# LayerNorms 1 to 3 carried through the projection that follows them

## What is computed

```python
def layer_norm(x, g, b):
    mu = mean(x); var = mean((x - mu) ** 2)
    return (x - mu) * rsqrt(var + 1e-5) * g + b

def conv_ffn(x, prev, w_up, w_dw, b_dw, w_down):
    g, v = split(x @ w_up, 2)
    g, new_prev = causal_dwconv(g, prev, w_dw, b_dw)
    return (gelu(g) * v) @ w_down, new_prev

# layer 0:  x = layer_norm(a*x + conv_module(x))       LayerNorm 0 inside, LayerNorm 1 here
#           x = layer_norm(a*x + conv_ffn(x))          LayerNorm 2
#           k, v = split(x @ w_kv)
# layer 1:  x = layer_norm(a*x + attention(x @ w_q, k, v) @ w_o)    LayerNorm 3
#           x = layer_norm(a*x + conv_ffn(x))          LayerNorm 4
```

## Time and profile before

| what | value |
|---|---|
| median of 3 runs | 2750.94 us (2749.96 to 2757.99) |
| span of the profiled execution | 2757.9 us (the slowest of the three runs: 2757.99 us) |
| PE busy | 2620.5 us, 95% |
| DVE busy | 1493.9 us, 54% |
| ACT busy | 1166.3 us, 42% |
| POOL busy | 274.9 us, 10% |
| mean granted TensorE clock | 0.969 |

### The profile page before, as it was taken

One profiled execution on the slowest core, in us unless ns is written; L12 is line 12 of the kernel. 1 busy time (PEld: TensorE's weight loads), 2 busy tenths in 40 slices (PEclk: granted clock), 3 DMA queues, 4 the chain that ended last, 5 costly groups with the idle time before them and its releaser, 6 DMA issues.

```text
span 2757.9 us, 48858 instructions
## 1 busy us (share of the span) xinstructions
PE 2620.5 (95%) x17562; PEld 2570.7 (93%) x17562; DVE 1493.9 (54%) x2187; ACT 1166.3 (42%) x1939; POOL 274.9 (10%) x224
## 2 busy tenths in 40 slices
PE   8889697999999999999989989899999999999996
PEld 7888597999999999999978979899999999999996
DVE  6888756544443344454466755654444334444555
ACT  7777635443332333343345433353343223443332
POOL 4888401000000000000010000100000000000001
PEclk9999798999999999999999968999999999999998
DMA  8444243444454344445433312434445434444542
GB/s 271 116 117 127 65 152 99 148 148 152 151 169 146 128 152 149 147 157 177 142 127 112 107 47 97 139 114 148 147 147 174 151 132 144 146 151 151 169 148 78
DMA packets 115061, 382.38 MB, mean 139 GB/s; under 512 B 29472, under 2 KB 29856, under 8 KB 114720
## 3 DMA queue, kind: packets, MB, share of 16 engines
q1 hardware_dynamic: 95328, 373.20, 41.4%
q0 software_dynamic: 992, 6.25, 0.6%
q10 hardware_dynamic: 18688, 2.21, 0.6%
HBM read 375.32 MB, written 8.27 MB: 139 GB/s over the span
## 4 chain that ended last, share of the span: by engine, by line
PE 85%; POOL 8%; DVE 3%; ACT 2%; issue 1%; POOLq 0%; DMA 0%; ACTq 0%; DVEq 0%; SPq 0%
PE acc L377 26%; PE acc L379 26%; PE acc L378 26%; POOL taps_pool L311 8%; PE acc L403 1%; PE acc L404 1%; PE acc L405 1%; DVE xr L1021 1%; ACT xr L728 1%; PE ot L665 0%; PE ot L667 0%; PE pt L564 0%; DVE rows L1034 0%; ACT xh L732 0%; PE pt L496 0%
## 5 line engine op out<-in xcount | busy, mean ns | idle before, releaser
L377 PE MATMUL acc<-xh,w_hi 128*128 128x320 f32 x3968 | 1236.1, 312 | 27.0 <-DVE w_lo L991 25.7
L379 PE MATMUL acc<-xh,w_lo 128*128 128x320 f32 x3968 | 1230.1, 310 | 0.0
L378 PE MATMUL acc<-xl,w_hi 128*128 128x320 f32 x3968 | 1229.7, 310 | 0.0
L685 ACT CAST w_hi<-w_raw 128x1024 fp32r<-128x1024 f32 (+1 forms) x648 | 699.0, 1117 | 556.2 <-PE acc L379 529.0
L991 DVE TENSOR_TENSOR w_lo<-w_raw,w_hi 128x1024 fp32r<-128x1024 f32 (+1 forms) x648 | 828.5, 1318 | 158.6 <-ACT w_hi L685 158.6
L377 PEld LDWEIGHTS acc<-xh,w_hi 128*128 128x128 f32 x3968 | 748.5, 189 | 41.9 <-DVE w_lo L991 32.4
L378 PEld LDWEIGHTS acc<-xl,w_hi 128*128 128x128 f32 x3968 | 748.6, 189 | 0.4
L379 PEld LDWEIGHTS acc<-xh,w_lo 128*128 128x128 f32 x3968 | 748.2, 189 | 0.0
L377 PE MATMUL acc<-hh,w_hi 128*128 128x320 f32 x1408 | 434.9, 309 | 0.0
L378 PE MATMUL acc<-hl,w_hi 128*128 128x320 f32 x1408 | 434.0, 308 | 0.0
L379 PE MATMUL acc<-hh,w_lo 128*128 128x320 f32 x1408 | 434.0, 308 | 0.0
(11 more groups left out here) (186 smaller groups left out, 1563.5 us busy)
## 6 DMA issues: line engine op xcount, KB each, us to landing
w_raw<-in_up SPq DMA_DIRECT2D x352, 512.0 KB, 4.3
w_raw<-in_down SPq DMA_DIRECT2D x128, 704.0 KB, 4.7
w_raw<-in_w_in SPq DMA_DIRECT2D x64, 512.0 KB, 5.9
w_raw<-in_w_out SPq DMA_DIRECT2D x32, 512.0 KB, 4.5
w_raw<-in_w_q SPq DMA_DIRECT2D x32, 512.0 KB, 4.8
w_raw<-in_w_o SPq DMA_DIRECT2D x32, 512.0 KB, 4.1
...
```

The costliest lines, as they stand in the source:

```text
L377: pe.matmul(out, wh, hi[:, k, :], start=first, stop=False)
L378: pe.matmul(out, wh, lo[:, k, :], start=False, stop=False)
L379: mm = pe.matmul(out, wl, hi[:, k, :], start=False, stop=last)
L685: act.copy(w_hi[:, slot, 0:n], w_raw[:, slot, 0:n]).then_inc(hi_ready, 1)
```

## The change

LayerNorms 1, 2 and 3 are no longer finished before the next projection starts. With m the mean and s = 1/std of a token, W(g(x - m)s + b) = s·W(gx) - m·s·Wg + Wb. So:

- While a residual projection runs, ACT and DVE already make the high and low part of z = g·x (with the shift taken off) for each finished tile (`z_hi`, `z_lo`). Two more columns of `xh` and `xl`, numbers 320 and 321, hold g and b (`const_columns`); the matmuls of the up projections, `w_kv` and `w_q` take 322 columns (`TX`) and so give Wg and Wb beside W·z.
- The next projection starts with `project_folded`: two whole groups instead of the batches, tile by tile behind `z_ready`. The two last moment matmuls go inside the first group, behind tiles 1 and 4.
- `norm_rows` makes only the rows `rstd` and `nmr` = -mean·rstd. Every evacuation applies them with the two columns (copied to `cols`): for gates on DVE and ACT through the tiles `gate_x` and `corr`, for values in two fused steps, for k, v and q in `w_kv` and `w_q`.
- The normalised x itself, which the residual needs later, is made by POOL while the next projection runs (`finish_norm`); the next residual addition waits for it (`x_normed`).
- Convolution and attention outputs get input tiles of their own (`conv_hi`, `conv_lo`, `attn_hi`, `attn_lo`), since `xh` and `xl` now hold z during `w_out` and `w_o`; LayerNorm 0 writes there and first waits until the convolution's state is stored. Dummy activations that load ACT's tables write to `table_out`. The scratch for POOL's DMA descriptors is set to 8192.

The core of the diff:

```diff
+TX = T + 2
...
-        xh = sb("xh", [P, KD, T], F32R)
-        xl = sb("xl", [P, KD, T], F32R)
+        xh = sb("xh", [P, KD, TX], F32R)
+        xl = sb("xl", [P, KD, TX], F32R)
...
+            def finish_norm(n):
+                g, b, l = FOLDED[n]
+                pool.wait_ge(rows_ready, n)
+                pool.wait_ge(z_ready, KD * n)
+                for q in range(4):
+                    lo, hi = 4 * q, 4 * q + 4
+                    at = 24 * (n - 1) + 6 * q
+                    pool.tensor_tensor(xr[:, lo:hi, :], xr[:, lo:hi, :], over_tiles(rstd, 4), ALU.mult
+                                       ).then_inc(x_normed, 1)
+                    pool.wait_ge(x_normed, at + 1)
+                    pool.tensor_tensor(xr[:, lo:hi, :], xr[:, lo:hi, :], over_tiles(nmr[:, :], 4), ALU.add
+                                       ).then_inc(x_normed, 1)
+                    pool.wait_ge(x_normed, at + 2)
+                    for k in range(lo, hi):
+                        pool.tensor_scalar(xr[:, k, :], xr[:, k, :], par(g)[:, k + KD * l, :], par(b)[:, k + KD * l, :],
+                                           ALU.mult, ALU.add).then_inc(x_normed, 1)
...
-            center(1, xr)
+            finish_norm(1)
...
-                    pe.matmul(out, wh, hi[:, k, :], start=first, stop=False)
+                    pe.matmul(out, wh, hi[:, k, 0:width], start=first, stop=False)
...
+                    if between and k in between:
+                        between[k]()
...
+            def project_folded(p, n, moments):
+                last_mean, last_square = moments
+                pe.wait_ge(const_cols_ready, n)
+                project_group(p, 0, 0, xh, xl, rhs_wait=(z_ready, KD * (n - 1)), width=TX,
+                              between={1: last_mean, 4: last_square})
+                project_group(p, 0, 1, xh, xl, width=TX)
...
-                        project_first_pair(up, xh, xl, event)
-                        project_pairs(up, xh, xl)
+                project_folded(up, n, moments)
+                project_pairs(up, xh, xl, width=TX)
...
-                pe.wait_ge(bank_read[par_], bank_count(p, pair))
+                pe.wait_ge(q_ready, t + 1)
...
+            def z_hi(n, k):
+                g, _, l = FOLDED[n]
+                act.wait_ge(shifted, KD * n + k + 1)
+                act.activation(xh[:, k, 0:T], xr[:, k, :], ACT.Identity, scale=par(g)[:, k + KD * l, :]
+                               ).then_inc(z_hi_ready, 1)
...
+                        act.wait_ge(cols_ready, 2 * tile + 1)
+                        act.activation(corr[:, :], nmr[:, :], ACT.Identity, bias=cols[:, 0, 1:2], scale=cols[:, 0, 0:1]
+                                       ).then_inc(corr_ready, 1)
+                        split_next(p, i, 0, end, chunks=(1,) if early else (0, 1))
+                        act.wait_ge(gate_ready, tile + 1)
...
+            def z_lo(n, k):
+                g, _, l = FOLDED[n]
+                dve.wait_ge(z_hi_ready, KD * (n - 1) + k + 1)
+                dve.scalar_tensor_tensor(xl[:, k, 0:T], xr[:, k, :], par(g)[:, k + KD * l, :], xh[:, k, 0:T],
+                                         ALU.mult, ALU.subtract).then_inc(z_ready, 1)
...
+            def norm_rows(n, nxt):
+                z_lo(n, KD - 1)
+                dve.wait_ge(moments_ready, n + 1)
+                dve.wait_ge(mean_squared, n + 1)
+                dve.tensor_tensor(rstd, ot[:, 0:T], work[:, 0, :], ALU.subtract).then_inc(var_ready, 1)
+                dve.wait_ge(std_ready, n + 1)
+                dve.reciprocal(rstd, rstd).then_inc(rstd_ready, 1)
+                dve.wait_ge(rstd_ready, n + 1)
+                dve.scalar_tensor_tensor(nmr[:, :], shift, -1.0, rstd, ALU.mult, ALU.mult).then_inc(rows_ready, 1)
+                split_lo(nxt, 0, 1, chunks=(1,))
+                dve.wait_ge(rows_ready, n)
...
-                        dve.tensor_tensor(work[:, 1, :], gy, acc[1][:, 0:T], ALU.mult).then_inc(bank_read[1], 1)
-                        split_next(p, i, 1, end)
+                        dve.tensor_copy(cols[:, 1, :], acc[1][:, T:TX]).then_inc(cols_ready, 1)
+                        dve.tensor_tensor(work[:, 1, :], acc[1][:, 0:T], rstd, ALU.mult).then_inc(bank_read[1], 1)
...
+                        split_next(p, i, 1, end)
```

More of the change, by code:

```diff
@@ L143, in trunk_kernel @@
             pass
-        with nc.sbuf_tensor("k_t", [P, 2, T], F32) as k_t, \
+        with nc.sbuf_tensor("conv_lo", [P, KD, T], F32R) as conv_lo, \
+                nc.sbuf_tensor("conv_hi", [P, KD, T], F32R) as conv_hi:
+            pass
+        with nc.sbuf_tensor("qo", [P, KD, T], F32) as qo, \
+                nc.sbuf_tensor("k_t", [P, 2, T], F32) as k_t, \
                 nc.sbuf_tensor("kc_t", [P, 2, NB, WINDOW], F32) as kc_t, \
@@ L154, in trunk_kernel @@
             pass
+        with nc.sbuf_tensor("attn_lo", [P, KD, T], F32R) as attn_lo, \
+                nc.sbuf_tensor("attn_hi", [P, KD, T], F32R) as attn_hi:
+            pass
         hh = sb("hh", [P, HALF, T], F32R)
         hl = sb("hl", [P, HALF, T], F32R)
+        gate_x = sb("gate_x", [P, T])
+        corr = sb("corr", [P, T])
         acc = [bank("acc0"), bank("acc1")]
@@ L233, in bank_count @@
             return p.base // 2 + ip + 1
[L236 removed]
+        RHS_X, RHS_CONV, RHS_ATTN = (NBT * e for e in range(3))
+        FOLDED = {1: ("mix_g", "mix_b", 0), 2: ("ffn_g", "ffn_b", 0), 3: ("mix_g", "mix_b", 1)}
         def over_tiles(row, n):
@@ L748, in _ @@
             split_hi(ph["w_in"], 1, 0, chunks=(0,))
-            act.activation(rstd[:, 0:1], shift[:, 0:1], ACT.Sigmoid)
+            act.activation(table_out[:, 0:1], shift[:, 0:1], ACT.Sigmoid)
             act.wait_ge(tables_loaded, 32)
@@ L811, in _ @@
             pairs(p, glu_and_square, first=2)
-            act.activation(rstd[:, 0:1], const("eps"), ACT.Sqrt)
+            act.activation(table_out[:, 0:1], const("eps"), ACT.Sqrt)
             act.wait_ge(products_summed, POOL_TAPS)
@@ L818, in _ @@
             conv_square(KD - 1)
-            norm(0, conv_y, ACT.Silu, "norm_g", "norm_b", 0, after[p.name], RHS_CONV)
+            act.wait_ge(state_saved, 16 * KD)
+            norm(0, conv_y, ACT.Silu, "norm_g", "norm_b", 0, after[p.name], RHS_CONV, conv_hi)
             def weights_only(p):
@@ L848, in body @@
                     square(n, 2 * ip + 1, xr[:, 2 * ip + 1, :], work[:, 1, :])
+                    if n in FOLDED:
+                        if end:
+                            last_z_hi(n, p)
+                        else:
+                            z_hi(n, 2 * ip + 1)
                 pairs(p, body, first=1)
             residual(ph["w_out"], 1)
-            norm(1, xr, ACT.Identity, "mix_g", "mix_b", 0, after["w_out"], RHS_MIX0)
+            norm_rows(1, after["w_out"])
             def ffn(l):
@@ L897, in _ @@
             ffn(0)
-            norm(2, xr, ACT.Identity, "ffn_g", "ffn_b", 0, after["down01"], RHS_FFN0)
+            norm_rows(2, after["down01"])
             weights_only(ph["w_kv"])
@@ L976, in _ @@
             for lo, hi in BATCHES:
-                act.copy(xh[:, lo:hi, :], qo[:, lo:hi, :]).then_inc(rhs_hi_ready, 1)
+                act.copy(attn_hi[:, lo:hi, :], qo[:, lo:hi, :]).then_inc(rhs_hi_ready, 1)
             residual(ph["w_o"], 3)
-            norm(3, xr, ACT.Identity, "mix_g", "mix_b", 1, after["w_o"], RHS_MIX1)
+            norm_rows(3, after["w_o"])
             ffn(1)
@@ L1217, in _, with ffn @@
             residual(ph["w_out"], 1.0, 1)
-            norm(1, xr, after["w_out"], RHS_MIX0)
-            def ffn(l, n_norm, rhs):
+            norm_rows(1, after["w_out"])
+            def ffn(l, n_norm):
                 if l:
@@ L1234, in body @@
                         gy_s = work[:, 0, SEQ:T].rearrange("p (n q) -> p n q", q=NQ)
+                        dve.wait_ge(multiplied, group_done(p, i, 0))
+                        dve.tensor_copy(cols[:, 0, :], acc[0][:, T:TX]).then_inc(cols_ready, 1)
+                        dve.tensor_tensor(gate_x[:, :], acc[0][:, 0:T], rstd, ALU.mult).then_inc(bank_read[0], 1)
+                        if not early:
+                            split_next(p, i, 0, end, chunks=(0,))
+                        dve.wait_ge(corr_ready, tile + 1)
+                        dve.wait_ge(bank_read[0], bank_count(p, i))
+                        dve.tensor_tensor(gate_x[:, :], gate_x[:, :], corr[:, :], ALU.add).then_inc(gate_ready, 1)
+                        split_next(p, i, 0, end, chunks=(1,))
                         dve.wait_ge(gate_taken, tile + 1)
-                        dve.scalar_tensor_tensor(gy[:, 1:SEQ], acc[0][:, 0:SEQ - 1], taps[:, 1:2], gy[:, 1:SEQ],
+                        dve.scalar_tensor_tensor(gy[:, 1:SEQ], gate_x[:, 0:SEQ - 1], taps[:, 1:2], gy[:, 1:SEQ],
                                                  ALU.mult, ALU.add).then_inc(taps_done, 1)
@@ L1410, in _ @@
             for bt in range(NBT):
-                rhs_lo(RHS_ATTN, bt, qo)
```

(7 more changed lines are left out.)

245 lines of the change are left out of this document (159 added, 86 removed).

## The result

The kernel before took 2752.86 us (median of 4 runs shown with the changed one), the changed kernel 2769.39. The ratio is 1.0062, with a 95% interval of 1.0044 to 1.0079: slower, where 2738.5 was forecast with a range of 2717 to 2768. The profiled execution has a span of 2774.3 us against 2757.9, in both kernels the slowest of four.

A forecast was written before the change was run, and what follows sets the result against it. PE was taken as the bound, busy 95% of the span. The terms -53.7 + 8.2 + 17.1 + 16, with 0 for the up loop, gave -12.4 us: 2745.5 profiled, 2738.5 as median, range 2717 to 2768.

The forecast's parts named there:

- The joints: Around LayerNorms 1 to 3, PE no longer waits between the residual projection and the next projection: -53.7 us.
- Two more columns: Matmuls of the up projections, w_kv and w_q take 322 columns instead of 320: +8.2 us, all on PE.
- columns in steps: Rival, 5%: 322 columns pay for another 32 column times in each widened matmul, 125 us more, about 2855 us.
- The evacuation in the up loop: Gate and value evacuations take more DVE work per pair, hidden by a slack of 2.3 us: 0 us.
- The evacuation of q: In w_q, a longer q evacuation puts 1.07 us more in front of PE in each of 16 groups: +17.1 us.
- POOL against DVE: POOL's normalising of x during the next projection holds up DVE instructions behind LayerNorms 1 to 3: +16 us (0 to 52).
- POOL and DVE starve PE: Rival, 20%: every quarter of POOL's work collides and PE's clock drops, 52 us together: +23.6, 2774.5 us.
- no collision: Rival, 24%: DVE's idle time takes in all of POOL's work after the LayerNorms: -28.4, 2722.5 us.

The follow-up runs named there:

- e7: The kernel before with the scores of q moved behind nine matmuls of the next w_q chunk; 2753.57 us, ratio 0.9994.
- e10: The kernel before, with POOL given the changed kernel's normalisation instructions on an unread spare buffer once the inputs of up00 and up10 are complete; 2764.1 us, ratio 1.0037.
- e11: As e10, but POOL's eight long passes read two different inputs; 2768.12 us in its one execution, beside 2757.76 of the kernel before.
- e4: The changed kernel with x normalised by DVE and ACT, tile by tile before each residual add, instead of POOL; 2735.30 us, ratio 0.9934.
- e5: The changed kernel with the scores of q moved behind nine matmuls of the next w_q chunk, POOL still normalising x; 2754.41 us, ratio 0.9999.
- e6: e4 with the scores of q moved behind nine matmuls of the next w_q chunk; 2717.05 us, ratio 0.9866.
- e2: The changed kernel with POOL's normalisation of x tile by tile, in passes of 128x320 instead of 128x1280; 2744.07 us, ratio 0.996.

## Why the prediction failed, step by step

**The joints, -53.7 us: right.** `w_out` gained 13.21 us and the first pair of `up00` 5.28 (20.61 to 15.33); `down01` 13.20 and the first pair of `w_kv` 2.97; `w_o` 13.66 and the first pair of `up10` 5.31: 53.6 us, by LayerNorm 18.5, 16.2 and 19.0 where 18.65, 16.34 and 18.68 stood. The clock in the first pair is 1.00. That they agree to 0.1 us is partly luck: forecast and ledger use the same execution of the kernel before, whose first pair of `up10` took 20.64 us there and 19.08 in e7.

**Two more columns, +8.2 us: mis-sized.** `up01` grew from 309.75 to 312.99 us: 3.24 / 2112 = 1.53 ns a matmul, not 0.83 to 0.92. For 8640 matmuls of the up projections and `w_kv` that is 13.2 us, and in `w_q` the spacing rose by 2.1 ns, 768 x 2.1 = 1.6: 14.9 us. I had no row of another width and took the ends from proportions; the rival of columns in steps asked the right question at the wrong size (block of 32 columns; the runs point to four).

**The evacuation in the up loop, 0 us: right where POOL is idle.** In `up01` and `up11` PE never waits. The slack of 2.3 us that made it free measures 2.39, but that is less than one of POOL's passes. I booked the slack here and the collisions in another term, as if they added; e10 and e11 show that they do not: POOL's passes cost 2.9 to 4.6 us a joint beside the unfolded loop, 15 beside the folded one.

**The evacuation of q, +17.1 us: right.** Ahead of 14 groups of scores the time from the last transpose's start to the first score matmul's rose from some 0.35 us to 1.41 to 1.49, 1.13 each. `w_q` without POOL's part is 241.56 - 222.36 = 19.2 us longer, and 1.6 of it are the columns: 17.6 us.

**POOL against DVE, +16 us: the step that failed.** Changed kernel minus e4, in `up00`, `w_kv`, `w_q` and `up10`: 15.0 + 1.3 + 7.3 + 14.8 = 38.3 us. Whole executions say nearly the same: e5 and e6, which differ only in who normalises x, lie 2754.41 - 2717.05 = 37.4 us apart. Three things in its working were wrong.
- I called 10.4 us per LayerNorm the end at which "nothing overlaps", and took half. Adding busy times bounds nothing when the waits lie in a chain: 4.40 + 5.75 us of waiting at PE and some 4.8 us of matmuls spaced wider at the lower granted clock (0.90 over that stretch) make the 15.0. The waits for `w_lo` came in two pairs behind each joint, not in four or five.
- POOL's steps were put down as "hardly stretched" by DVE, from three passes in a stretch where DVE did little. In fact, behind LayerNorm 1, POOL took 44.6 us (455.56 to 500.2), not 35: the tensor_scalars took 1.06 us in the mean over the run, not 0.6. At the end of LayerNorm 2's work four of them take 2.38 us together, 0.6 each, as estimated for POOL alone:

```profile
1450.05 2.38 POOL L352 TENSOR_SCALAR xr<-xr,params 128x320 f32<-128x320 f32 x4
```

- At the start of `w_q` I reckoned with two passes met, 6 us; 8.6 came, 1.3 of it in `w_kv`. The first q chain itself met one pass after another, in steps of 0.35 and 0.25 us (DVE, then POOL):

```profile
1444.29 2.85 DVE L1493 TENSOR_SCALAR q_st<-q_raw,cols 128x256 f32<-128x256 f32 x1
1447.06 2.93 DVE L1494 TENSOR_SCALAR q_s<-q_raw,cols 128x64 f32<-128x64 f32 x1
...
1443.88 3.10 POOL L345 TENSOR_TENSOR xr<-xr,rows 128x1280 f32<-128x1280 f32 x1
1447.07 2.88 POOL L348 TENSOR_TENSOR xr<-xr,nmr 128x1280 f32<-128x1280 f32 x1
```

The Trainium skill ("SBUF — State Buffer", "SBUF: two separate sides") says that either engine can block the other for a whole instruction. The traces agree in both directions (2.93 us for 0.25 on DVE here, 2.83 for 0.7 on POOL in e2, there behind three instructions of DVE). The 10.4 us that I drew from that rule was my sum of busy times, not the rule's.

**The whole.** -53.6 + 14.9 + 17.6 + 38.3 = +17.2, less 0.4 for the columns in three first pairs, which already stand in the joints: +16.8 us, against 16.4 between the spans. Of the 29 us between the forecast's -12.4 and +16.4, POOL's term holds 22.3 and the columns 6.7. What came is the rival "POOL and DVE starve PE": it decides from 28.4 us of collisions on, and they were 38.3. That its 2774.5 us is so near to 2769.4 is partly luck: its 52 us were 13.7 too many, and half of that the columns made up. Its dips of the clock were too many and too short, 12 at 1.6 us; four came in `up00` and `up10`, some 2.4 us each. It had 20%, too little: the subtract of 2.61 us in the earlier trace rows, at five times its own 0.49, was a reason for more. The range's lower end is a slip as well: no collision with both cheap ends gives 2750.94 - 53.7 + 7.8 + 15 = 2720, not 2717; nothing else hangs on it.
